# Down products of both MLPs: seven block products for a pair of output tiles and both token halves, weight sums on GpSimd

## The reference, cut to what matters

```python
def mlp(h, w_up, w_down):
    return jnp.square(jax.nn.relu(h @ w_up)) @ w_down
xp = xp + mlp(rmsnorm(xp, norm_mlp_g[layer]), w_up[layer], w_down[layer])
```

## Time and profile before

| | |
|---|---|
| three runs | 1791.98, 1792.21, 1797.71 us (median 1792.21) |
| profiled execution | known by its span, 1793.1 us; no time beside it is given |
| TensorE busy | 1736.8 us, 97% |
| VectorE busy | 954.7 us, 53% |
| ScalarE busy | 548.6 us, 31% |
| GpSimd busy | 159.4 us, 9% |
| first MLP, unbroken piece | 399.81 to 796.82 us |
| second MLP, unbroken piece | 1383.09 to 1780.11 us |

### The profile page before, as it was taken

How to read it: one execution, slowest core, us unless ns; L and a number is a source line. 1 busy time by engine, 2 the same in 40 slices (tenths; PEclk the granted TensorE clock), 3 DMA queues, 4 the chain that set the end, 5 groups by cost and what they waited for, 6 DMA issues and landing times.

```text
span 1793.1 us, 36785 instructions
## 1 busy us (share of the span) xinstructions
PE 1736.8 (97%) x15035; PEld 1623.3 (91%) x15035; DVE 954.7 (53%) x1454; ACT 548.6 (31%) x1075; POOL 159.4 (9%) x212
## 2 busy tenths in 40 slices
PE   7998999999999999999999999999999999999998
PEld 6995667899999999999898898878799999999998
DVE  4336776655353433444587774677665435343454
ACT  4114556432121222231511413443133212122222
POOL 0710000320000000020000000012012000000002
PEclk9999999999999999999999999999999999999999
DMA  8219999337676767544368678523033767422221
GB/s 277 71 50 363 351 353 346 124 118 257 234 257 234 257 233 257 187 131 158 96 198 284 211 253 274 197 83 102 33 121 120 278 227 260 173 79 88 75 91 55
DMA packets 167162, 338.82 MB, mean 189 GB/s; under 512 B 9178, under 2 KB 116500, under 8 KB 165437
## 3 DMA queue, kind: packets, MB, share of 16 engines
q1 hardware_dynamic: 164691, 249.74, 41.3%
q0 software_dynamic: 2240, 87.41, 13.0%
q10 hardware_dynamic: 114, 0.03, 0.0%
HBM read 324.36 MB, written 100.19 MB: 237 GB/s over the span
## 4 chain that ended last, share of the span: by engine, by line
PE 86%; DVE 7%; ACT 2%; DMA 2%; issue 1%; SPq 1%; ACTq 0%; DVEq 0%
PE pp L667 55%; PE pp L977 16%; PE pp L727 2%; PE pp L926 1%; DMA kvring<-in_cache_b_kv 1%; PE pp L741 1%; PE pp L761 1%; PE pp L1084 1%; PE pp L1131 1%; PE pp L1180 1%; PE pp L1109 1%; DVE stat L1668 1%; DVE pp L1666 1%; ACT e_p L2163 1%; DMA vring<-in_cache_d_kv 1%
## 5 line engine op out<-in xcount | busy, mean ns | idle before, releaser
L1943 ACT ACTIVATE whi<-raw 128x1024 fp32r<-128x1024 f32 x208 | 220.6, 1060 | 899.7 <-PE pp L667 687.7
L667 PE MATMUL pp<-a_hi,whi 128*128 128x288 f32 x1280 | 275.8, 297 | 1.0 <-DVE zbuf L1335 0.7
L667 PE MATMUL pp<-a_lo,whi 128*128 128x288 f32 x1280 | 274.6, 296 | 0.0
L667 PE MATMUL pp<-a_hi,wlo 128*128 128x288 f32 x1280 | 274.4, 296 | 0.0
L1292 DVE TENSOR_TENSOR wlo<-raw,whi 128x1024 fp32r<-128x1024 f32 x208 | 256.0, 1231 | 30.5 <-ACT whi L1943 30.4
L667 PE MATMUL pp<-b_hi,whi 128*128 128x288 f32 x1152 | 247.0, 296 | 0.0
L667 PE MATMUL pp<-b_lo,whi 128*128 128x288 f32 x1152 | 247.0, 296 | 0.0
L667 PE MATMUL pp<-b_hi,wlo 128*128 128x288 f32 x1152 | 246.9, 296 | 0.0
L1351 DVE TENSOR_TENSOR x<-x,pp 128x576 f32 (+1 forms) x80 | 60.4, 755 | 295.1 <-PE pp L667 284.0
L667 PEld LDWEIGHTS pp<-a_hi,whi 128*128 128x128 f32 x1280 | 206.6, 189 | 2.3 <-issue 1.7
L667 PEld LDWEIGHTS pp<-a_lo,whi 128*128 128x128 f32 x1280 | 206.7, 189 | 0.0
(11 more groups left out here) (304 smaller groups left out, 2062.9 us busy)
## 6 DMA issues: line engine op xcount, KB each, us to landing
kvring<-in_cache_b_kv SPq DMA_DIRECT2D x128, 512.0 KB, 5.6
out_new_d_sample<-in_cache_d_kv POOLq DMA_DIRECT2D x32, 2040.0 KB, 8.5
raw<-in_w_up SPq DMA_DIRECT2D x32, 1024.0 KB, 5.4
raw<-in_w_down SPq DMA_DIRECT2D x32, 1024.0 KB, 5.2
kring<-in_cache_d_kv SPq DMA_DIRECT2D x104, 256.0 KB, 3.3
vring<-in_cache_d_kv SPq DMA_DIRECT2D x104, 256.0 KB, 5.3
raw<-in_w_in_cd SPq DMA_DIRECT2D x24, 1024.0 KB, 5.2
out_new_d_sample<-in_cache_d_kv POOLq DMA_DIRECT2D x8, 2016.0 KB, 8.3
```

Of the source, the lines that this page charges most:

```text
L667: last = pe.matmul(acc_h[s][:, h, :], w[s][:, k, :], m[:, k, NH * h:NH * h + NH], start=(at_ == 0 and n == 0), stop=(at_ == KT_N - 1 and n ...
L1943: act.activation(whi_v[j], raw_v[q // 2][:, :, j, :], ACT.Copy).then_inc(whi_ready, 1)
```

## The change

The down part of a chunk is computed as 4 **pairs** of output tiles (i = 0 to 3). For a pair, the weights are four blocks: a11, a12, a21, a22 of 4 k steps x 128 columns. The first number tells the output tile and the second the half of k. The squares are b11, b12 (first half of k, token halves) and b21, b22. Seven products of 4 k steps x 3 parts = 12 matmuls (p = 0 to 6, m = 7i + p from 0 to 27) replace eight block products. Their operands are blocks or sums. For the weights there are four sums, made by GpSimd: a11-a21, a21+a22, that less a11, and a12 less the last. For the squares there are four differences, made by VectorE: t1 = b12-b11, t2 = b22-t1, t3 = b22-b12, t4 = b21-t2. Operands are split in high and low parts after summing: seven forms of the squares (`bf_hi`, `bf_lo`), and a weight form for each product (`f_hi`, `f_lo`, 6 slots).

Three PSUM accumulators hold running sums over products; VectorE reads one after each product and adds it to a quarter of two tiles of `x` (`read`). TensorE starts product m when form m is there and the read of product m-2 is done. Weight form m+6 is made when product m is done. In the first four products the last k step is put off until the squares of the last up tile are there. The tiles of an up part and their split are as before. The counters now run 36 to a chunk (8 + 28) in place of 16. GpSimd's copies of caches keep their order and stand in one list with the sums. The last chunk finishes the tiles of `x` in pairs, 6 and 7 both at the end. Elsewhere in the kernel only counter values change, and four semaphores become two.

```diff
T_AB, T_OA, T_M0 = 0, 16, 24
-T_CD = T_M0 + 64
+CHUNK, DOWN = 36, 28
+T_CD = T_M0 + 4 * CHUNK
 T_OC = T_CD + 48
 T_M1 = T_OC + 8
-T_END = T_M1 + 64
+T_END = T_M1 + 4 * CHUNK
+LOADS = {T_M0: T_M0 // 4, T_CD: T_M0 // 4 + 16}
+LATE = T_CD // 4 - LOADS[T_CD]
+LOADS[T_M1] = T_M1 // 4 - LATE
+PRODUCTS = ((None, 0, 0), (2, 5, 2), (1, 4, 0), (None, 2, 1), (0, 1, 0), (None, 6, 2), (3, 3, 0))
+SUM_READY = (2, 3, 1, 4)
+SLOT = [(m + 4) % 6 for m in range(24)] + [4, 5, 2, 3]
+FORM_AFTER = {m: m + 6 for m in range(20)} | {22: 26, 23: 27}
...
+        raw_q = [t[:, :].rearrange("p (k e j n) -> p k e j n", k=4, e=2, j=2) for t in raw]
+        w_sum = [[at(f"w_sum{i}{n}", W_S + 2048 * i + 512 * n, 512)[:, :].rearrange("p (k n) -> p k n", k=4)
+                  for n in range(4)] for i in range(2)]
...
+        sq_h = [sqbuf[:, N * j:N * j + N].rearrange("p (h c) -> p h c", h=2) for j in range(2)]
+        A_BANK, B_BANK, C_BANK = (bank[0][:, 0:NH], bank[3][:, 0:NH]), bank[2][:, 0:NH], bank[1][:, 0:NH]
...
+        def weight_form(m):
+            i, p = m // 7, m % 7
+            n = PRODUCTS[p][0]
+            if n is not None:
+                return w_sum[i % 2][n]
+            e, j = {0: (0, 0), 3: (1, 0), 5: (1, 1)}[p]
+            return raw_q[i % 2][:, :, e, j, :]
+        def product_bank(m):
+            i, p = m // 7, m % 7
+            return (A_BANK[i % 2], C_BANK, B_BANK)[PRODUCTS[p][2]]
+        B_BASE = (8, 16 + 80)
...
             def mlp_weights(L, t0):
                 up, down = a["w_up"][L], a["w_down"][L].rearrange("(c k) n -> c k n", c=4)
...
+                def chunk(c, first):
+                    for v in range(4):
+                        before = (first, 0, 2, 4)[v]
+                        sp.wait_ge(wlo_ready, in_chunk(t0, c, before))
+                        sp.dma_start(raw_v[v % 2].rearrange("p k j n -> p k (j n)"),
+                                     up.rearrange("(k p) n -> p k n", p=P)[:, :, ds(c * 1024 + 256 * v, 256)]
+                                     ).then_inc(raw_loaded[v % 2], 16)
+                    for i in range(4):
+                        sp.wait_ge(wlo_ready, in_chunk(t0, c, (6, 8, 8 + 7, 8 + 14)[i]))
+                        sp.dma_start(raw_v[i % 2].rearrange("p k j n -> p k (j n)"),
+                                     down[ds(c, 1), :, 256 * i:256 * i + 256]
+                                     .rearrange("o (k p) n -> p (o k) n", p=P)).then_inc(raw_loaded[i % 2], 16)
+                chunk(0, -2)
+                with sp.Fori(1, 4) as c:
+                    chunk(c, -7)
...
             def mlp(L, t0):
-                G0, fa, fb = t0 // 4, 8 * (1 + 2 * L), (8, 48)[L]
-                dense(lambda i: i + G0, 2, ahk, alk, a_ready, fa, hook=mean_square(1 + 2 * L), peel=True)
-                dense(lambda i: i + (G0 + 2), 2, bhk, blk, b_ready, fb)
+                def up_tile(c, u, first):
+                    pe.wait_ge(wlo_ready, in_chunk(t0, c, u + 1))
+                    pe.wait_ge(acc_free, in_chunk(t0, c, u + 1))
...
+                def steps(m, ks):
+                    p = m % 7
+                    f, s_ = PRODUCTS[p][1], SLOT[m]
+                    for k in ks:
+                        for n, (w, b) in enumerate(((f_hi_v, bf_hi), (f_hi_v, bf_lo), (f_lo_v, bf_hi))):
+                            last = pe.matmul(product_bank(m), w[s_][:, k, :], b[:, f, k, :],
+                                             start=(k == 0 and n == 0 and p in (0, 1, 3)),
+                                             stop=(k == 3 and n == 2), skip_group_check=(p in (2, 4, 5, 6)))
+                    return last
+                def down(c):
+                    w_ready = lambda m: pe.wait_ge(wlo_ready, in_chunk(t0, c, 8 + m + 1))
+                    reads = lambda m: pe.wait_ge(acc_free, in_chunk(t0, c, 8 + m + 1))
+                    squares = lambda n: pe.wait_ge(b_ready, c * 20 + (B_BASE[L] + 15 + n))
+                    w_ready(0)
+                    reads(0)
+                    squares(1)
+                    steps(0, range(4)).then_inc(tile_done, 1)
+                    w_ready(1)
+                    reads(1)
+                    steps(1, range(3))
+                    w_ready(3)
+                    steps(3, range(3))
+                    reads(2)
+                    steps(2, range(3))
+                    squares(4)
+                    for m in (1, 2, 3):
+                        steps(m, (3,)).then_inc(tile_done, 1)
+                    squares(5)
+                    for m in range(4, DOWN):
+                        w_ready(m)
+                        reads(m)
+                        steps(m, range(4)).then_inc(tile_done, 1)
+                for u in range(8):
+                    up_tile(0, u, u == 0)
+                    if u == 0:
+                        mean_square(1 + 2 * L)()
+                down(0)
                 with pe.Fori(1, 4) as c:
-                    dense(lambda i: c * 4 + (i + G0), 2, ahk, alk, a_ready, fa)
-                    dense(lambda i: c * 4 + (i + (G0 + 2)), 2, bhk, blk, b_ready, c * 8 + fb)
+                    for u in range(8):
+                        up_tile(c, u, False)
+                    down(c)
...
+                def form_lo(m, c):
+                    dve.wait_ge(whi_ready, in_chunk(t0, c, 8 + m + 1))
+                    dve.tensor_tensor(f_lo_v[SLOT[m]], weight_form(m), f_hi_v[SLOT[m]].bitcast(F32),
+                                      ALU.subtract).then_inc(wlo_ready, 1)
+                def tile_lo(c, u):
+                    dve.wait_ge(whi_ready, in_chunk(t0, c, u + 1))
+                    dve.tensor_tensor(wlo_v[u % 2], raw_v[u // 2 % 2][:, :, u % 2, :], whi_v[u % 2].bitcast(F32),
+                                      ALU.subtract).then_inc(wlo_ready, 1)
+                def read(m, c):
+                    i, p = m // 7, m % 7
+                    j, h = ((0, 0), (1, 1), (1, 0), (0, 0), (1, 1), (1, 0), (0, 1))[p]
+                    at_ = (2 * i + j) * N + NH * h
+                    dve.wait_ge(tile_done, in_chunk(t0, c, 8 + m + 1))
+                    if p in (3, 4, 5):
+                        dve.wait_ge(acc_free, in_chunk(t0, c, 8 + m - 3 + 3))
+                    dve.tensor_tensor(x[:, at_:at_ + NH], x[:, at_:at_ + NH], product_bank(m),
+                                      ALU.add).then_inc(acc_free, 1)
+                def squares_lo(c, kk, n, forms, src):
+                    dve.wait_ge(bhi_ready, c * 20 + (bb + 5 * kk + n))
+                    dve.tensor_tensor(bf_lo[:, forms, kk, :], src, bf_hi[:, forms, kk, :].bitcast(F32),
+                                      ALU.subtract).then_inc(b_ready, 1)
+                def up_tile(c, u, first):
+                    j, kk = u % 2, u // 2
+                    z = zbuf[:, N * j:N * j + N]
+                    dve.wait_ge(tile_done, in_chunk(t0, c, u + 1))
+                    if first:
+                        rms(1 + 2 * L)(t0 // 4, 2)
+                    dve.tensor_tensor(z.rearrange("p (h c) -> p h c", h=2), acc_h[j], r_h, ALU.mult).then_inc(acc_free, 1)
+                    dve.wait_ge(acc_free, in_chunk(t0, c, u + 3))
+                    if j == 0:
+                        dve.wait_ge(b_ready, c * 20 + (bb + 5 * kk))
+                    dve.scalar_tensor_tensor(out=sqbuf[:, N * j:N * j + N], in0=z, scalar=0.0, in1=z, op0=ALU.max,
+                                             op1=ALU.mult).then_inc(sq_up, 1)
+                    dve.wait_ge(sq_up, c * 8 + (32 * L + u + 1))
+                    made = c * 16 + (64 * L + 4 * kk)
+                    b11, b12, b21, b22 = sq_h[0][:, 0, :], sq_h[0][:, 1, :], sq_h[1][:, 0, :], sq_h[1][:, 1, :]
+                    t1, t2, t3, t4 = (b_sum[:, n, :] for n in range(4))
+                    if j == 0:
+                        dve.tensor_tensor(t1, b12, b11, ALU.subtract).then_inc(b_sums, 1)
+                        if u < 6 and not first:
+                            tile_lo(c, u + 2)
+                        squares_lo(c, kk, 1, 0, b11)
+                        squares_lo(c, kk, 2, 1, t1)
+                        if u == 6:
+                            for m in range(4):
+                                form_lo(m, c)
+                        return
+                    dve.wait_ge(b_sums, made + 1)
+                    dve.tensor_tensor(t2, b22, t1, ALU.subtract).then_inc(b_sums, 1)
+                    dve.tensor_tensor(t3, b22, b12, ALU.subtract).then_inc(b_sums, 1)
+                    if u < 7:
+                        tile_lo(c, u + 2)
+                    squares_lo(c, kk, 3, slice(2, 4), sq_h[1])
+                    dve.wait_ge(b_sums, made + 2)
+                    dve.tensor_tensor(t4, b21, t2, ALU.subtract).then_inc(b_sums, 1)
+                    if u == 7:
+                        read(0, c)
+                    squares_lo(c, kk, 4, slice(4, 6), b_sum[:, 1:3, :])
+                    squares_lo(c, kk, 5, 6, t4)
...
+                def chunk(c, first=False, last=False):
```

(84 more changed lines are left out.)

199 lines of the change are left out of this document (107 added, 92 removed).

## The result

The changed kernel takes 1814.88 us (median of four runs, 1811.87 to 1817.1) beside 1792.26 us for the kernel before. The ratio is 1.0118, with a 95% interval of 1.0099 to 1.0136: slower by 1.2%, where 1782 us and 0.6% faster had been forecast. The profiled execution took 1817.1 us, its span is 1815.5 us.

A forecast was written before the change was run, and what follows sets the result against it. TensorE, busy for 97% of the span, was taken as the bound: 1793.1 - 51.2 (removed matmuls) + 37.6 (seams) + 2 (ends) = 1781.5, said as 1782 us, with a range for 8 in 10 of 1755 to 1808.

The forecast's parts named there:

- Removed matmuls: Down parts of both MLPs: 384 matmuls go at 0.1334 us each, 51.2 us less.
- The seam undisturbed: Up tile 7 to product 4, without GpSimd's sums: TensorE waits 1.5 us per seam for VectorE's read of product 2.
- The seam with sums: Up tile 7 to product 4: GpSimd's sums delay VectorE, so TensorE waits 4.7 us per seam, 37.6 us in all.
- the alternation: At the seam, GpSimd's sums get in between VectorE's four low weights: read of product 2 at 11.6 us, result 1785.5.
- rival (b): After seam waits from about 1.9 us TensorE's clock falls: 1802 us, at most 1810; chance 0.29.
- The landing of weights: Down part: weight blocks of pairs 2 and 3 land with margins of 4 us and more; cost taken as 0.
- What stands behind a waiting instruction: Down part: GpSimd's bursts for pairs 2 and 3 cost 0 to 0.3 us each, taken as 0; ScalarE's squares there unmentioned.
- The ends: End of each MLP: one more square sum behind the last product; 2 us together, from 0 to 4.
- The three signs: Prediction wrong if GpSimd's sums take over 1.5 us each, the steady down part has waits, or the clock falls.
- Rival (a): At seams GpSimd's sums don't meet VectorE's chain: one wait of 1.5 us each, 1756 us (1764 with 2.5); chance 0.29.
- rival (c): TensorE loses 0.2 us in each of 28 products of 6 looped quarters, 34 us more: 1815 us; chance 0.04.

The follow-up runs named there:

- the best version: Changed kernel with all weight sums on VectorE, those of pairs 2 and 3 one product later, ScalarE's squares late, two cache copies after the last chunk's product 12: 1770.05 us.

## Why the prediction was wrong, step by step

**Removed matmuls: right.** 51.2 us had been taken. Without sums a down part is 45.1 us plus its wait, against 51.1: 6.0 x 8 = 48. The matmuls kept their pace of 0.133 us; the 3 us that are missing lie at the eight stops, 0.3 us or so each beyond the idle time shown.

**The seam undisturbed: right.** 1.5 us predicted, 1.62 found, at the read of product 2, in every quarter.

**The seam with sums: the mechanism was right, its turn wrong, its waits too long.** I had 4.7 us each, 37.6 in all. The waits are 4.0 us each, 32 in all; only the slow clock behind them brings the seams to about 44. I had read rows 8 as GpSimd being kept out of a back-to-back run on VectorE, and let the sums start after the four low forms. In fact one got in between each two, and the first wait of TensorE was for the eviction of tile 7, which the prediction had in time. The Trainium skill, "SBUF — State Buffer", section "SBUF: two separate sides", says that whichever starts first holds the shared ports for its whole instruction; the trace agrees, with low forms 1.7 us apart in place of 0.6. I had named that rule and set it aside on one row. As it was priced in the prediction (the alternation gives 1785.5) this alone would have cost 4 us. The price of a sum was wrong too. I had taken 1.04 us for two of the four because both inputs lie in one tile. None of the 128 sums took less than 1.25 us, and the mean was 1.56 to 1.67 by line. The kernel before already had an undisturbed addition within one tile at the higher price:

```profile
87.38 1.31 POOL L2381 TENSOR_TENSOR pool_a<-pool_a 128x512 f32<-128x512 f32 x1
```

So one tile or two is not what sets the price; what does was not tried.

**The clock: the rival (b) was partly right.** It gave 1802 for this cause alone. The last column of the table is 17.3 us over eight quarters, of which about 12 lie behind the seams, and the end of the kernel ran at 0.50 too. I had made the forecast and (b) exclude each other, and put the clock at nothing in the forecast. With waits of 2.0 and 2.25 us in each seam of my own forecast, a part of it belonged in the sum.

**The landing of weights: the failed step, and the largest single miss.** The prediction took "margins of 4 us and more" and put the loss at nothing. The margin was taken from the median landing, 5.2 us; the row gave 15.4 as its longest. In the second MLP's second quarter a load took 17.0 us, TensorE waited 6.36 us for it and 2.3 us in what followed, and with the slow clock behind this the loss is 12 us; the run with the copies moved gives 12.2 back.

**What stands behind a waiting instruction: not seen.** For the last quarters I looked at TensorE and VectorE, not at ScalarE's squares, which wait for GpSimd and stand ahead of the high forms. This was put at nothing and is about 9 us in both MLPs. 5 come back in the trace when the squares are moved; for the other 4 no cause is shown.

**The ends: too small.** 2 us taken, 4 the bound; the part behind the last product is 5.3 us longer, with waits of 0.45 and 1.55 us and the clock at 0.50 behind them. It is still 17.0 in the best version, which also finishes two tiles together; how much of it that is was not tried by itself.

Together, over the forecast of 1781.5 for a span that became 1815.5, which is 34.0: about 6 for the seams with their clock, 12 for the load, 9 for the last quarters, 3 at the ends, 3 for the matmuls (48 us gone where I had 51.2), and about 1 unassigned. The three signs that the prediction gave for being wrong all came: sums over 1.5 us, waits in the steady down part, and a clock that falls. Rival (a), no meeting at the seam, is what moving the sums to VectorE brings about; rival (c), 0.2 us more for each of 28 products or 5.6 us a quarter, is refuted by the quarters without sums at 45.1 us for 336 matmuls.

## What to carry to other kernels

An engine that looks idle is not free if its instructions hold up those of the engine that the critical one waits for: the same additions cost 25 us more on GpSimd than on VectorE, which is busy for 69% of the changed kernel and for 70% of the version in which it makes these sums itself. When a change cuts a buffer's lead, compare the new margin with the longest landing in the trace, not the median, and look at what else is in flight there. And follow each in-order queue past the instruction that waits: twice here (squares, landing) the cost lay behind it.
